# Context row tiles of the expert sum: scaled by ScalarE, added up by GpSimd, one TensorE step per run of 16

## The reference

```python
def _peer(h, wq, subkeys, u_tab, v_tab):        # for each block of 128 tokens xt
    ...
    expert = jnp.take_along_axis(cand_i, best_p, axis=-1)      # 8 heads x 16 of 16384 experts
    g = jax.nn.softmax(best_s, axis=-1)
    act = jax.nn.gelu(jnp.einsum('thkd,td->thk', u_tab[expert], xt).astype(jnp.float32))
    wgt = (g * act).astype(xt.dtype)
    return jnp.einsum('thk,thkd->td', wgt, v_tab[expert]).astype(xt.dtype)
```

## Time and profile before

| | |
|---|---|
| median of three runs | 4582.91 us (4581.86 to 4584.9) |
| the profiled execution | 4594.0 us, its span 4592.2 us |
| TensorE busy with matmuls | 3765.4 us (82%) |
| VectorE busy | 2791.6 us (61%) |
| ScalarE busy | 1640.2 us (36%) |
| GpSimd busy | 1630.2 us (35%), 1623.9 us of it in 1280 gathers |
| DMA | 1672.71 MB, mean 364 GB/s |

### The profile page before, as it was taken

One profiled execution on the slowest core, in us unless ns is written; L12 is line 12 of the kernel. 1 busy time (PEld: TensorE's weight loads), 2 busy tenths in 40 slices (PEclk: granted clock), 3 DMA queues, 4 the chain that ended last, 5 costly groups with the idle time before them and its releaser, 6 DMA issues. The chain is left out here.

```text
span 4592.2 us, 44497 instructions
## 1 busy us (share of the span) xinstructions
PE 3765.4 (82%) x12065; PEld 1571.8 (34%) x12065; DVE 2791.6 (61%) x6341; ACT 1640.2 (36%) x5133; POOL 1630.2 (35%) x1312
## 2 busy tenths in 40 slices
PE   7999999999998789999876887888777556666676
PEld 6654455656553223443321231332222111111110
DVE  1122777577675976655898566555588985544444
ACT  4211345232112443334344333333434553333333
POOL 0000133223222333333344434443444445565554
PEclk9999999999999889999886997999877676666666
DMA  8645688789999989999998989999999999999998
GB/s 342 234 158 208 267 331 325 275 304 389 362 370 386 373 340 402 376 385 403 404 393 326 422 347 405 403 397 408 403 402 389 396 393 416 415 421 415 414 422 350
DMA packets 267834, 1672.71 MB, mean 364 GB/s; under 512 B 29184, under 2 KB 46656, under 8 KB 89792
## 3 DMA queue, kind: packets, MB, share of 16 engines
q0 software_dynamic: 184320, 1342.26, 73.0%
q1 hardware_dynamic: 75104, 304.18, 17.1%
q10 hardware_dynamic: 8160, 23.43, 1.6%
HBM read 1631.98 MB, written 37.78 MB: 364 GB/s over the span
## 5 line engine op out<-in xcount | busy, mean ns | idle before, releaser
L1075 POOL DMA_INDIRECT slots<-in_peer,idxR x1280 | 1623.9, 1269 | 2886.6 <-PE ps L1380 1801.4
L1380 PE MATMUL ps<-slots,lhs 128*64 128x512 f32 x4544 | 1499.2, 775 | 707.0 <-ACT lhs L1130 704.5
L1665 DVE CUSTOM_DVE_ANT_0 slots<-slots,h2R 128x1024 f32<-128x1024 f32 x1280 | 1546.7, 1224 | 752.6 <-issue 687.5
L1364 PE MATMUL ps<-ring,arena 128*128 128x512 f32 (+2 forms) x4300 | 1557.8, 520 | 34.7 <-DMA ring<-in_wa 8.0
L1364 PEld LDWEIGHTS ps<-ring,arena 128*128 128x128 f32 x4300 | 788.5, 196 | 830.4 <-issue 778.9
L1380 PEld LDWEIGHTS ps<-slots,lhs 128*64 128x64 f32 x4544 | 297.3, 159 | 1802.6 <-ACT lhs L1130 1570.9
L1119 ACT ACTIVATE gelus<-dots 128x1 f32<-128x1 f32 x1280 | 256.4, 200 | 1508.0 <-DVE dots L1665 1505.8
L1130 ACT ACTIVATE lhs<-fold,wgts 128x64 f32<-128x64 f32 x1136 | 395.2, 348 | 37.2
L1122 ACT ACTIVATE wgts<-gelus,gsmR 128x1 f32<-128x1 f32 x1280 | 377.0, 295 | 42.3 <-ACT gelus L1119 0.5
L1364 PE MATMUL ps<-ring,slots 128*128 128x512 f32 (+1 forms) x704 | 249.1, 515 | 0.0
L1677 DVE SCALAR_TENSOR_TENSOR slots<-slots,wgts 128x1024 f32<-128x1024 f32 x135 | 173.1, 1282 | 88.0 <-ACT wgts L1122 82.0
(11 more groups left out here) (202 smaller groups left out, 2255.3 us busy)
## 6 DMA issues: line engine op xcount, KB each, us to landing
ring<-in_whead SPq DMA_DIRECT2D x24, 2048.0 KB, 11.3
ring<-in_wa SPq DMA_DIRECT2D x24, 2048.0 KB, 10.8
ring<-in_wq SPq DMA_DIRECT2D x16, 2048.0 KB, 19.9
slots<-in_peer,idxR POOLq DMA_INDIRECT x1280, 12.6
ring<-in_wgc SPq DMA_DIRECT2D x16, 1024.0 KB, 9.8
ring<-in_wgb SPq DMA_DIRECT2D x8, 2048.0 KB, 11.4
ring<-in_wout SPq DMA_DIRECT2D x8, 2048.0 KB, 21.8
o_scratch<-inb SPq DMA_DIRECT2D x80, 128.0 KB, 5.2
```

The lines of the kernel that those rows point to most:

```text
L1075: g.indirect_dma_start(out=slot(R), out_offset=None, in_=a["peer"], in_offset=bass.IndirectOffsetOnAxis(ap=idxR[:, p % KEEP, g2, col:col + ...
L1364: done = mm(out, lhsT, rhs, start=n == 0, stop=n == len(pairs) - 1)
L1380: done = mm(ps[j * HALF:(j + 1) * HALF, g2, :], weights, slot(R)[:, D + j * UW:D + (j + 1) * UW], start=start, stop=stop)
L1665: v.tensor_tensor_reduce(out=u, in0=u, in1=h2R[:, g2, :], scale=1.0, scalar=0.0, op0=ALU.mult, op1=ALU.add, accum_out=dots[:, R % LHS:R % ...
```

## The change

`Plan` gets a second set, `pooled`: the tiles below the first chained one (0 to 79) and the context tiles above the last chained one (224 to 255), 112 in all, seven runs of 16. For these tiles ScalarE no longer writes `lhs`; it multiplies v, 128x1024, by the tile's weight in its slot. GpSimd adds the slot before to the slot for each tile but a run's first, four tiles behind its gathers (POOL_LAG), and waits for ScalarE's product (`w_done`) and for its own last addition. TensorE takes each run's last slot with `fold`. A slot of a pooled tile comes free when the addition that reads it is done (`pool_sum_done`); that of a run's last tile still when TensorE is done. VectorE's instructions stay as they are.

```diff
--- before.py
+++ after.py
@@ -44,7 +44,7 @@
 KEEP = 6
 ROWS = P
 NR = NC * ROWS
-ACT_LAG, VEC_LAG, PE_LAG = 1, 2, 3
+ACT_LAG, VEC_LAG, PE_LAG, POOL_LAG = 1, 2, 3, 4
 RUN = 16
 DEEP = 12
 RANK_LAG = 3
@@ -555,17 +555,23 @@
         for R in range(0, len(placed) - RUN, RUN):
             if placed[R] >= first and placed[R + RUN - 1] < last:
                 self.chained.update(range(R, R + RUN))
-        self.by_pe, self.by_vec = [0], [0]
+        self.pooled = set(range(min(self.chained) // RUN * RUN)) | set(range(max(self.chained) + 1, BASE[1] * ROWS))
+        self.by_pe, self.by_vec, self.by_pool = [0], [0], [0]
         for R in range(NR):
             self.by_vec.append(self.by_vec[-1] + (R in self.chained))
-            self.by_pe.append(self.by_pe[-1] + (R not in self.chained or self.chain_end(R)))
-
-    def chain_end(self, R):
-        return R in self.chained and R % RUN == RUN - 1
+            self.by_pool.append(self.by_pool[-1] + (R in self.pooled and R % RUN > 0))
+            self.by_pe.append(self.by_pe[-1] + self.on_pe(R))
+
+    def in_run(self, R):
+        return R in self.chained or R in self.pooled
 
     def on_pe(self, R):
 
-        return R not in self.chained or self.chain_end(R)
+        return not self.in_run(R) or R % RUN == RUN - 1
+
+    def pool_rows(self, R):
+
+        return self.by_pool[R + 1]
 
     def pe_rows(self, R):
 
@@ -789,6 +795,7 @@
             m8_out m8_in mod_done pk_done modd_out lng_in subk_in psc_in pw_in hT_out hg_in state_in state_out
             sm_done state_done zero_done zv_done sq_done ms_done std_done x_done tmp_free gate_done in_free
             h2_done gm_in cond_done top_done exp_done sum_inv gsm_done idx_done dot_done w_done row_free sum_done
+            pool_sum_done
             acc0_free acc1_free gt2_in yx_in y_sum y_sq y_ms y_std y_done y_out
             act_step dve_step pool_step""".split()
         s = {n: sem(n) for n in names}
@@ -836,6 +843,8 @@
 
             if plan.on_pe(R):
                 eng.wait_ge(s["row_free"], plan.pe_rows(R))
+            elif R in plan.pooled:
+                eng.wait_ge(s["pool_sum_done"], plan.pool_rows(R + 1))
             else:
                 eng.wait_ge(s["sum_done"], plan.vec_rows(R) + 1)
 
@@ -1062,6 +1071,14 @@
             st.settle()
             pool.sem_inc(s["mask_done"], 1)
 
+            def add_up(R):
+
+                here, before_it = slot(R)[:, D:2 * D], slot(R - 1)[:, D:2 * D]
+                pool.wait_ge(s["w_done"], R + 1)
+                if R % RUN > 1:
+                    pool.wait_ge(s["pool_sum_done"], plan.pool_rows(R) - 1)
+                g.tensor_tensor(here, here, before_it, ALU.add).then_inc(s["pool_sum_done"], 1)
+
             for R in range(NR):
                 p, g2, pair, col, head = row_of(R)
                 if R == 0:
@@ -1076,6 +1093,8 @@
                     out=slot(R), out_offset=None, in_=a["peer"],
                     in_offset=bass.IndirectOffsetOnAxis(ap=idxR[:, p % KEEP, g2, col:col + 1], axis=0),
                 ).then_inc(row_in[plan.slot(R)], 16)
+                if R - POOL_LAG in plan.pooled and (R - POOL_LAG) % RUN:
+                    add_up(R - POOL_LAG)
 
         @block.scalar
         def _(eng):
@@ -1123,6 +1142,11 @@
                              scale=gsmR[:, p % KEEP, g2, col:col + 1])
                 if R in plan.chained:
                     weights.then_inc(s["w_done"], 1)
+                    return
+                if R in plan.pooled:
+                    st.link(weights)
+                    here = slot(R)[:, D:2 * D]
+                    A_(here, here, ACT.Copy, scale=wgts[:, n:n + 1]).then_inc(s["w_done"], 1)
                     return
                 st.link(weights)
                 if R >= LHS:
@@ -1371,6 +1395,9 @@
                 weights = lhs[:, R % LHS, :]
                 if R in plan.chained:
                     pe.wait_ge(s["sum_done"], plan.vec_rows(R))
+                    weights = fold[:, :]
+                elif R in plan.pooled:
+                    pe.wait_ge(s["pool_sum_done"], plan.pool_rows(R))
                     weights = fold[:, :]
                 else:
                     pe.wait_ge(s["w_done"], R + 1)
```

## The result

The changed kernel takes 4671.73 us in the median of four runs (4670.45 to 4676.63), against 4583.37 for four of the kernel before (one more than the three of the table above): a ratio of 1.0194, 95% interval 1.0178 to 1.0210, some 89 us. The profiled execution took 4671.9 us, 78 us more than the profiled one of before (4594.0), so the two traces differ by 78 us; the profiled execution of before lies 11 us above its median.

The account below looks back on a forecast made before the run. GpSimd was to replace TensorE as the bound: +36 in A, +7 in B and +5 for late groups sum to +48, taking the profiled 4594.0 to 4642, less 11 to the median: 4631 us, range 4535 to 4725.

Parts of the forecast that it names:

- TensorE removed: Over A and B, 105 tiles leave TensorE, about 0.99 us each in A, 1.09 in B: 105 us in all.
- A: Stretch of tiles 6 to 79, 525.10 to 793.76 us, 268.7 us long, TensorE the bound; forecast 305 us, +36.
- The addition: On GpSimd, 105 two-input additions of 128x1024, taken as 2.13 us each, between bounds of 0.95 and 4.3.
- The gap: On GpSimd, 0.30 us with each addition, because the next gather must see the addition done.
- B: Stretch of tiles 228 to 255, 1435.18 to 1543.40 us, 108.2 us long, DMA engines at 0.98; forecast 115 us, +7.
- I take 0.3 us for bad alignment.: Wait per addition from VectorE's two-input steps, whose 1.72 us a tile just fit GpSimd's 1.73 us between additions.
- ScalarE: Its 128x64 write becomes a 128x1024 product, 0.70 us more a tile; no bound in A, costed at nothing.
- Clock: TensorE rests more, so projection groups run slower after idle time; three late groups on the path, +5 (0 to 20).
- The loop of five: From a gather to the gather five later: 13.4 us needed against 20 us available, so no bound, 6 us in hand.
- The signs that I had named: Profile marks for right or wrong, such as TensorE some 60% busy in A, tile 80's gather some 36 us later.
- Rival 1: GpSimd's addition is short or disturbs nobody, and VectorE is next to bound: -42, 4541 us; chance 0.24.
- Rival 3: Each addition and each VectorE dot wait for one another in full: +137, 4720 us; chance 0.12.

Follow-up runs that it names:

- memset kernel: Changed kernel with each GpSimd addition replaced by a write of zeros over the slot's 2048 columns; ratio 1.0019 to the kernel before, 9 us slower.
- wait_only: Changed kernel whose GpSimd keeps the waits for ScalarE's products but adds nothing, slots freed one tile later; ratio 0.9948 to the kernel before, 24 us faster.
- no_add: Changed kernel without GpSimd's additions or their waits, a slot free once scaled; ratio 0.9932 to the kernel before, 31 us faster.

## Why the prediction was right in kind and half in size

The forecast was 4631 us, +48 on 4583, with a range of 4535 to 4725; 4671.7 lies in it. The sign and GpSimd's part in it came as said. The terms:

- **TensorE removed**: 83 us less busy in place of 105; the rest is most likely the lower clock (0.81 in A in place of 0.97), at which remaining matmuls are longer (the scan's L1513 takes 482 ns in A, and took 429). It does no harm to the sum, since it is idle time anyway.
- **The addition**, taken as 2.13 us between bounds of 0.95 and 4.3: 2.44 in the mean, 2.36 in the median. The Trainium skill, page "GPSIMD Engine Reference", section 3.1, gives 4497 ns for 2048 columns; half of it, an estimate, is 2.25, and the measurement is a little above it.
- **The gap**, taken as 0.30 us from gather to gather: 0.77 in front of a gather that waits for the addition just ahead, as in nearly all of A, and 0.16 with eight slots, as in B. With the 0.77 and the addition, an addition costs GpSimd 3.23 us with its gaps (2.44, 0.77, 0.02) where I had 2.43 before port waits. GpSimd's own series in A is then 74 x 1.17 + 70 x 3.23 = 313 us: +44 of the +81 by the gathers, where I had 276 without the 0.3 us and the run ends. The 2.44 already holds what VectorE cost the additions, 0.08 us each over the median.
- **The step that failed: "I take 0.3 us for bad alignment."** I asked only how long GpSimd would be held, and fitted VectorE's 1.72 us a tile into the 1.73 us that GpSimd leaves. But nothing in the kernel puts VectorE's steps into that window; they run into the addition and stand there: its busy time in A rose by 96 us (211 to 307), with steps that I hadn't counted, of one small input, among them (the first of the two index splits, from 170 to 701 ns). What is over in A beyond GpSimd's own series, 81 - 44 = 37 us, I put down to this hold, passed on through ScalarE: GpSimd stood 31.6 us for ScalarE's products, and another 6.8 for TensorE. That split of the 81 is read from waits, not tried. The experiment gives the hold, at equal GpSimd time and with the shorter additions of 768 columns, 47 us over both stretches, where the forecast had 29.
- **B**, taken as +7: +22 by the marks, +30 alone. I priced only GpSimd's time there. VectorE was busy 89.2 of 139 us in the window that I read the earlier trace rows, but 104.5 of 115 from 1495 to 1610 us; this dense part begins inside the window that I read (41.8 of 48 us up to 1543) and runs on behind its end. Between the marks at 1457 and 1563 us of before, the changed kernel loses 24 us, that with 768 columns 15 and the memset kernel 2: most of it is VectorE's hold.
- **ScalarE**, costed at nothing: +15 alone. The six banks that I named as cover hold the projections' results; TensorE's row tiles wait for ScalarE's step itself, which is now longer.
- **Clock**, +5: not separated. The clock did fall, but with TensorE at 63% in A it is unlikely to bind.
- **The loop of five**, with 6 us in hand, taken as no bound: wait_only has the same order and look-ahead with no work in them, and by the medians it is 7 us slower than no_add. With the held dots in the loop it was not tried alone.
- **GpSimd's waits before.** I read that GpSimd stood 216.1 of 264 us for TensorE; 43.55 of these lie in front of 525 us. No term uses it.
- **The signs that I had named.** Of those for being right, TensorE's share (63%), the additions' length and the longer dots came; tile 80's gather came 83 us later and not 36. Of those for being wrong, one came in part: GpSimd idle behind ScalarE's products, 31.6 us in A, which I had said would point to VectorE, and it did. B's gathers took 32 us more, over the 30 that I had tied to the shorter look-ahead, but wait_only, with that look-ahead, loses nothing between the marks at 1457 and 1563 us (it gains 1 us), which clears it.
- **Rival 1** said -42 if the addition were free: -31. **Rival 3** (4720) was the rule at its worst; the result lies halfway from the forecast to it, and its mechanism is the one that the runs show, though a dot in A lost 0.52 us in the mean and not 1.23.

The ladder, each step the difference of two kernels, with the sum so far behind it: ScalarE's product +15 (+15); TensorE relieved -46 (-31); the order of the queue, up to 7, and 1.82 us of GpSimd time a tile, together +40 (+9); the same time spent reading, +47 (+55, by rounding); 0.54 us more of it, +33 (+89). This last step is at once more time on GpSimd and a longer hold on VectorE, and was not split.

## What to carry to other kernels

Before you give an idle engine work, ask which of its neighbours it stops, and put the price on the neighbour too: GpSimd had 65% of its time free, but its additions stopped VectorE's steps, and VectorE was the next bound at 92%. A relief of a bound engine is worth no more than the room on the next one (31 us in this case where 105 us of TensorE's work went, with the new additions free of charge), so read the second-busiest engine of the dense parts first. Where VectorE itself has room, let it do the addition: the run of 64 to 79 on VectorE was 16 us faster than before, on GpSimd 6.

## What the hardware showed beyond what was expected

- A GpSimd addition of two 128x1024 SBUF tiles takes 2.36 us in the median, 128x768 1.82, 128x512 1.27; a gather that must see it done starts 0.77 us later and one that need not, 0.16, where gathers follow each other in 0.30.
- A VectorE step that met an addition was held until the addition ended, even one of 128x2 (0.17 to 1.80 us), and two additions back to back held a dot through both (3.31 us for one of 1.23).
- A GpSimd write of 128x2048, 1.82 us, did not hold the dot: it stays at 1.225 us, and VectorE's busy time over the span is 6 us above that of before, where 768 columns of addition in the same time add 82.
- ScalarE's product with a column of weights, 128x1024 in place, takes 1149 ns; its 128x1024 step without such a column took 1047.
